# Attention's search spread in unequal parts over a step, and four buffers where the experts' rows are added

## The chip, the cores and the metric

One core of one Trainium2 chip runs the whole kernel. The metric is the time of one execution on the device in microseconds; lower is better. Three runs of the kernel before took 6582.45, 6589.72 and 6597.27 us; the median is 6589.72 us.

## What is computed

A prompt of 2048 tokens and eight sample tokens go through two layers of width 1024. Layer 0 has sparse attention: an indexer gives each query a score for each key, the best 256 keys are chosen (ties go to the earlier key), and attention runs over those alone. Layer 1 is a recurrent block. Behind each stands a mixture of 32 experts of which each token uses two. Only two places matter here:

```python
def block(args):                       # 128 queries of the prompt at a time
    sc = indexer_scores(qib, wib, ki, q_pos, k_pos)      # relu(q.k) per head, weighed, masked
    _, idx = lax.top_k(sc, topk)                         # topk = 256 keys
    valid = idx <= q_pos[None, :, None]
    return sparse_attend(qb, gather_rows(k, idx), gather_rows(v, idx), valid)

# the end of the experts: each token adds its two experts' rows
return jnp.zeros((N, D), x.dtype).at[st].add(yb[dest] * sw[:, None])
xp = xp + g2p[:, None, :] * hier_moe(...)                # both layers
y_prompt = rmsnorm(xp, norm_final_g)                     # behind the last
```

## The kernel before

The phases follow each other with a barrier of all engines between them: modulation, project, attend, the samples' index and attention, and then for each layer route, experts, combine, with the recurrent block between the layers. The change touches `phase_attend` (L485) and `phase_combine` (L2130).

**Attention** (`phase_attend`). The 16 tiles of 128 queries are taken in the order `TILE` (0, 1, 3, 5, ..., 15, 14, 12, ..., 2), so tile m has `L[m]` keys, 128 to 2048 and back to 384. The work is a pipeline written out by hand over `steps()`: in step i the engines do four tiles at once.

- Tile i: the attention proper. A step has `slots(i)` slots (2 to 32), each with two blocks of 128 keys for four heads. On TensorE `biased` and `scored_by_keys` (L952, L959) write scores, ScalarE takes the exponential (`exponentials`, L715), TensorE multiplies with the values one slot later (`with_values`, L970).
- Tile i+1: the row maxima. TensorE's `fill` (L980, L981) adds the hiding mask `hide` to a head's scores in one of two banks of `aux`, VectorE's `largest` (L795) reduces them. These units are shared over the first half of the slots, up to `middle(i)`.
- Tile i+2: the search for the 256th score. `cand` is found bit by bit in 31 rounds. For tiles of 1024 keys and more (`by_act`) ScalarE counts with a Sign and an accumulator (`weigh`, L752), and VectorE answers with the next bit (L848, L850); a round needs the answer of the one before. For narrower tiles VectorE counts itself (L835, L892, L894). Round 32 settles the last bit for ScalarE's tiles, and then `finish_search` (L896 to L919) counts the ties with a scan (L913) and writes `hide`. GpSimd copies it (`split_hide`, L664) for the step in which the tile is tile i.
- Tile i+3: the indexer's scores. TensorE's `index` (L1020) writes a pair of pieces into the two banks of `aux`, ScalarE rectifies them (L747) into one of four buffers, VectorE adds them up (L827). The pairs are shared over the second half of the slots.
- Tile i-1: the end. In the second slot VectorE's `normalise` (L807, L809) turns 1024 row sums per partition into reciprocals and multiplies; in the slot `middle(i)` TensorE projects (L992) and GpSimd adds the residual.

Before the change the 33 rounds are shared evenly over all slots of the step, and `finish_search` is one call behind the last round, in the last slot. Each engine works through its own list in the order in which the Python code writes it. In a slot TensorE does: scores, half of the units, values of the slot before, the other units, the projection in the slot `middle(i)`, and then the pairs. At the end of a step `turn_queries` (L1027) turns the queries of tile i+2, ScalarE copies them (L761) and GpSimd narrows them into `qTb` (`narrow`, L692), which the next step's units read together with `hide`. VectorE does in a slot: units, `normalise`, pairs, rounds.

**Combine** (`phase_combine`). For each of 17 tiles of tokens (the last has 8) GpSimd gathers two rows of 4 KB per token from `yb` (`indirect_dma_start`, L2186), SyncE loads `x` (L2171), ScalarE scales the first row (L2208), VectorE adds the second, multiplies with the gate and adds `x` (L2233, L2235, L2237), and ScalarE's queue stores `z` (L2204). `x`, `y` and `z` have two buffers. In layer 1 (`final`) the norm follows: ScalarE squares (L2215), GpSimd takes the root (`norm_rstd`, L246 and L247, with a `drain` between them) and VectorE multiplies (L2243). GpSimd's order in a turn of the loop is

```python
copy of the two indices into idxb, wait for it
gather(t, 0); gather(t, 1)
norm(t - 1)            # final only: add, drain, pow
```

In layer 0 SyncE first loads `rec_w_out` (4 MB), then the gates, then the `x` tiles.

## Time and profile before

| what | us |
|---|---|
| median of three runs | 6589.72 |
| profiled execution | 6591.56 |
| its span, first to last instruction | 6590.1 |
| attention's steps 0 to 15 (from 728 to 3008) | 2280 |
| combine of layer 0 (from 4339 to 4493) | 154 |
| combine of layer 1 (from 6384 to the end) | 206 |

The profile is one execution, taken by the hardware. A page of it lists busy time by engine and groups of instructions; the trace behind it can be asked for stretches (busy time of each engine in a window), for the order of events (timeline), and for groups with their waits. In a row PE is TensorE, PEld its weight loads, DVE VectorE, ACT ScalarE, POOL GpSimd, SP SyncE. "[5.35 <-DVE attend_mx L795]" is the time that the engine stood idle before the row and what ended it.

### The profile page before, as it was taken

The numbers are of one execution on the slowest core, as the hardware profiler recorded it, in microseconds if no ns is written. First come the engines' busy times: TensorE is split into PE (matmuls) and PEld (weight loads), VectorE is DVE, ScalarE is ACT, GpSimd is POOL, SyncE is SP. The second block draws the span as 40 slices with busy tenths as digits, with TensorE's granted clock in tenths as the row PEclk, the third lists the DMA queues.
The fourth block names the chain that finished last, engine by engine and source line by source line (L and its number), as shares of the span: only waits on it lengthen the run. The fifth ranks groups of instructions, "written<-read, shape, count | busy, mean of one in ns | idle before, by whom it ended". The sixth has DMA issues, their size and how long they took to land. (4 is left out here: it accounts for less than half of the span.)

```text
span 6590.1 us, 58804 instructions
## 1 busy us (share of the span) xinstructions
PE 4886.5 (74%) x16399; PEld 2498.9 (38%) x16453; DVE 2284.1 (35%) x4967; ACT 1865.8 (28%) x3244; POOL 696.1 (11%) x934
## 2 busy tenths in 40 slices
PE   7999456676787888887775599924888886579960
PEld 2444122222233333333234444413566564544430
DVE  1111554454345545653122301124444442321114
ACT  0111224455555553321121112212222231212211
POOL 0111211000000001111121100021000000100013
PEclk9999577888899999998886699966988896589985
DMA  6111100000000000004442677752000100447865
GB/s 239 52 49 37 53 12 16 10 8 12 12 5 12 7 12 12 15 19 150 128 150 88 245 284 280 261 210 95 32 25 19 38 13 17 147 140 272 292 217 163
DMA packets 177185, 634.10 MB, mean 96 GB/s; under 512 B 28920, under 2 KB 47737, under 8 KB 157930
## 3 DMA queue, kind: packets, MB, share of 16 engines
q1 hardware_dynamic: 112124, 408.37, 17.8%
q0 software_dynamic: 39072, 131.90, 6.0%
q10 hardware_dynamic: 25824, 91.88, 3.5%
q8 instruction: 74, 1.21, 0.1%
q14 instruction: 91, 0.75, 0.0%
HBM read 497.41 MB, written 134.72 MB: 96 GB/s over the span
## 5 line engine op out<-in xcount | busy, mean ns | idle before, releaser
L2112 PE MATMUL experts_ps_gu<-w_sb,experts_xT 128*128 x1504 | 679.6, 606 | 42.7 <-DMA w_sb<-moe_w_in 38.2
L970 PE MATMUL attend_po<-attend_PT,V 128*128 128x512 f32 x1088 | 564.8, 644 | 30.9 <-ACT attend_PT L715 18.5
L752 ACT ACTIVATE attend_passed<-attend_score,attend_cand 128x1024 bf16<-128x1024 f32 (+8 forms) x279 | 439.3, 1575 | 468.2 <-DVE attend_cand L850 443.9
L2621 PE MATMUL recurrent_psAB<-recurrent_hT,rec_w_in_sb 128*128 128x256 f32 (+1 forms) x2304 | 537.1, 393 | 10.6 <-ACT recurrent_hT L2416 10.6
L469 PE MATMUL project_pj<-project_w,project_hT 128*128 128x512 f32 (+2 forms) x1360 | 507.5, 530 | 6.6 <-ACT project_proj L385 5.5
L2621 PEld LDWEIGHTS recurrent_psAB<-recurrent_hT,rec_w_in_sb 128*128 128x128 f32 x2304 | 464.5, 215 | 77.1 <-issue 11.7
L795 DVE TENSOR_REDUCE attend_mx<-attend_aux 128x1 f32<-128x512 f32 (+3 forms) x640 | 365.3, 606 | 289.8 <-PE attend_aux L981 283.3
L2112 PEld LDWEIGHTS experts_ps_gu<-w_sb,experts_xT 128*128 128x128 f32 x1504 | 285.3, 195 | 372.0 <-issue 372.0
L981 PE MATMUL attend_aux<-attend_KTb,attend_qTb 128*128 128x512 bf16 (+3 forms) x640 | 236.2, 376 | 214.5 <-issue 198.3
L715 ACT ACTIVATE attend_PT<-attend_big 128x512 f32<-128x512 f32 x544 | 291.3, 586 | 238.9 <-PE attend_big L959 238.0
L2102 PE MATMUL experts_ps_y<-w_sb,experts_midT 128*128 x752 | 343.3, 600 | 11.4 <-issue 11.4
L959 PE MATMUL attend_big<-attend_qT,KT 64*128 64x512 f32 x1088 | 338.2, 701 | 0.0
L980 PE MATMUL attend_aux<-attend_hide,attend_identb 128*128 128x512 bf16 (+3 forms) x587 | 215.5, 371 | 162.4 <-DVE attend_mx L795 150.8
L970 PEld LDWEIGHTS attend_po<-attend_PT,V 128*128 128x128 f32 x1088 | 208.8, 205 | 317.2 <-issue 244.9
L469 PEld LDWEIGHTS project_pj<-project_w,project_hT 128*128 128x128 f32 (+1 forms) x1360 | 229.4, 185 | 261.7 <-issue 254.6
L1020 PE MATMUL attend_aux<-kiT,attend_qiT 64*128 64x512 f32 (+3 forms) x640 | 197.6, 701 | 160.8 <-ACT attend_relu L747 136.1
L980 PEld LDWEIGHTS attend_aux<-attend_hide,attend_identb 128*128 128x128 bf16 x640 | 64.2, 101 | 615.5 <-DVE attend_mx L795 337.2
L2066 DVE SCALAR_TENSOR_TENSOR experts_th<-experts_th,experts_ps_gu 128x256 f32<-128x256 f32 x94 | 39.6, 421 | 734.2 <-ACT experts_th L2045 734.2
L827 DVE SCALAR_TENSOR_TENSOR attend_score<-attend_relu,attend_wi,attend_score 128x512 f32<-128x512 f32 (+3 forms) x280 | 187.5, 671 | 282.3 <-ACT attend_relu L747 265.4
L2652 PE MATMUL recurrent_psO<-rec_w_out_sb,recurrent_g 128*128 128x512 f32 (+1 forms) x544 | 238.6, 599 | 28.6 <-DVE recurrent_g L2578 28.6
L992 PE MATMUL attend_aux<-attend_w_out,attend_oT 128*128 128x512 f32 x512 | 227.5, 603 | 16.5 <-DVE attend_oT L809 16.5
L2045 ACT ACTIVATE experts_th<-experts_ps_gu 128x256 f32<-128x256 f32 x94 | 36.0, 383 | 678.7 <-PE experts_ps_gu L2112 678.7
(426 smaller groups left out, 6124.3 us busy)
## 6 DMA issues: line engine op xcount, KB each, us to landing
w_sb<-moe_w_in SPq DMA_DIRECT2D x64, 2048.0 KB, 11.4
w_sb<-moe_w_in SPq DMA_DIRECT2D x64, 1024.0 KB, 8.8
yb_scratch<-experts_y ACTq DMA_DIRECT2D x94, 512.0 KB, 8.6
index_slab<-ada_w_in SPq DMA_DIRECT2D x12, 2048.0 KB, 9.6
sample_V<-cache_v_in POOLq DMA_DIRECT2D x128, 128.0 KB, 2.4
sample_K<-cache_k_in SPq DMA_DIRECT2D x128, 128.0 KB
route_x<-xa_scratch SPq DMA_DIRECT2D x32, 512.0 KB, 4.5
hs_scratch<-route_h ACTq DMA_DIRECT2D x32, 512.0 KB, 4.8
```

Of the source, the lines that this page charges most:

```text
L469: last = pe.matmul(pj[0:rows, bank, 0:c1 - c0], hT[:, b, k, 0:rows], w[:, k, c0:c1], start=(k == 0), stop=(k == KC - 1))
L715: act.activation(PT[:, g % 4, :], big[:, g % 4, :], ACT.Exp).then_inc(exped, 1)
L752: act.activation(passed[:, 0:L[m]], score[:, m % 2, 0:L[m]], ACT.Sign, bias=threshold, accum_out=balance[:, :]).then_inc(balanced, 1)
L795: dve.tensor_reduce(mx[:, h, c:c + 1], aux[:, u % 2, 0:wide], AX.X, ALU.max).then_inc(maxed, 1)
L959: pe.matmul(big[:, g % 4, :], KT[r, n // 2, b * P:(b + 1) * P], qT[r, i % 3, n // 2 * GQ:(n // 2 + 1) * GQ, :].rearrange("p a q -> p (a q) ...
L970: pe.matmul(po[:, n % 2, :], V1[:, b, n, :], PT[:, g % 4, :], start=(b == 0), stop=(b == S[i] // NKV - 1)).then_inc(pv_done, 1)
L980: pe.matmul(aux[:, u % 2, 0:n], identb4[:, 0, :], hide[:, keys], start=True, stop=False)
L981: pe.matmul(aux[:, u % 2, 0:n], qTb[:, h, :], KTb[:, h // GQ // 2, keys], start=False, stop=True).then_inc(unit_filled, 1)
L2102: last = pe.matmul(ps_y[:, half, :], midT[:, k, :], w2[:, bass.ds(slot, 1), k, half * 512:half * 512 + 512].rearrange("p a n -> p (a n)"), ...
L2112: last = pe.matmul(ps_gu[:, u, :], xT[:, u, k, :], w1[:, bass.ds(slot, 1), k, :].rearrange("p a n -> p (a n)"), start=(k == 0), stop=(k == ...
L2621: last = pe.matmul(psAB[:, c % 2, part, 0:W], w_in[:, k, part * D + c * P:part * D + (c + 1) * P], hT[:, k, 0:W], start=(k == 0), stop=(k ...
L2652: last = pe.matmul(psO[0:rows, half, :], g[:, k, i * P:i * P + rows], w_out[:, k, half * 512:half * 512 + 512], start=(k == 0), stop=(k == ...
```

## The change

In attention the rounds get unequal weights over a step's slots (two in the first half, one in the second, none in the last slot or two), `finish_search` becomes four pieces of its own, `normalise` becomes five parts spread over the first half, and TensorE writes half of a slot's pairs ahead of the values. In combine the buffers go from two to four, the loops are written out, the copy of the indices goes, SyncE stores as well as loads, and GpSimd's root of tile t comes ahead of the gathers of tile t+4.

```diff
-        ROUNDS = 33
+        PIECES = 37
+        def pieces_at(i, s):
+            n = slots(i)
+            if not there(i + 2):
+                return range(0)
+            weight = [1] if n == 1 else [2 if k < middle(i) else 1 for k in range(n - 1)] + [0]
+            if n > 8:
+                weight[n - 2] = 0
+            done, of = sum(weight[:s]), sum(weight)
+            return range(PIECES * done // of, PIECES * (done + weight[s]) // of)
+
+        def normal_at(i, s):
+            if middle(i) <= 2:
+                return range(5) if s == min(1, middle(i)) else range(0)
+            return share_of(5, s, 1, middle(i))
...
-                            for r in share_of(ROUNDS, s, 0, slots(i)):
+                            for r in pieces_at(i, s):
                                 if r < 31:
                                     weigh(i + 2, r)
...
-                def normalise(i):
+                def normalise(i, part):
                     dve.wait_ge(o_copied, 16 * (i + 1))
-                    dve.reciprocal(total[:, :, :], total[:, :, :])
-                    dve.drain()
-                    dve.tensor_tensor(oT[:, :, :], oT[:, :, :], total[:, :, :], ALU.mult).then_inc(o_normed, 1)
+                    if part < 4:
+                        dve.reciprocal(total[:, 2 * part:2 * part + 2, :], total[:, 2 * part:2 * part + 2, :])
+                    else:
+                        dve.drain()
+                        dve.tensor_tensor(oT[:, :, :], oT[:, :, :], total[:, :, :], ALU.mult).then_inc(o_normed, 1)
...
                 def search(m, r):
-                    if by_act(m):
+                    if r > 32:
+                        finish_search(m, r - 33)
+                    elif all_chosen(m):
+                        return
+                    elif by_act(m):
                         search_with_act(m, r)
...
+                def finish_search(m, part):
...
+                    elif part == 0:
+                        if m:
+                            dve.wait_ge(split_done, 2 * m)
+                            dve.wait_ge(unit_filled, sum(U[:m]))
+                        counted(m, threshold, ALU.is_gt)
+                        dve.tensor_scalar(out, at, threshold, None, ALU.is_equal)
+                        dve.tensor_scalar(count[:, :], count[:, :], -float(TOPK), None, ALU.add)
+                    elif part == 1:
+                        dve.drain()
+                        dve.tensor_tensor_scan(passed[:, 0:w], out, out, count[:, 0:1], ALU.add, ALU.bypass)
+                    elif part == 2:
+                        dve.drain()
+                        dve.scalar_tensor_tensor(out, passed[:, 0:w], 0.0, out, ALU.is_gt, ALU.mult)
+                    else:
+                        dve.drain()
+                        dve.scalar_tensor_tensor(out, at, threshold, out, ALU.is_lt, ALU.add)
+                        dve.drain()
+                        dve.tensor_scalar(out, out, -BIG, None, ALU.mult).then_inc(hidden, 1)
...
-                        units = units_at(i, s)
+                        units, pairs = units_at(i, s), pairs_at(i, s)
+                        early = 0 if s == middle(i) else (len(pairs) + 1) // 2
                         for u in units[:len(units) // 2]:
                             fill(i + 1, u)
+                        for pair in pairs[:early]:
+                            index(i + 3, pair)
                         if s:
                             with_values(i, 2 * s - 2)
                             with_values(i, 2 * s - 1)
...
-                        for pair in pairs_at(i, s):
+                        for pair in pairs[early:]:
                             index(i + 3, pair)
```

```diff
+    DEEP = 4
-        idxb = sb("idxb", [P, 2, 2], I32)
+        x = sb("x", [P, DEEP, D])
+        y = sb("y", [P, DEEP, 2, D])
+        z = sb("z", [P, DEEP, D])
...
             @block.sync
+                def store(t, b, rows):
+                    sp.wait_ge(done if final else added, t + 1)
+                    out = (T["y_prompt"][t * P:t * P + rows] if rows == P else T["y_sample"]) if final else rows_at(dst, t, rows)
+                    sp.dma_start(out, z[0:rows, b, :]).then_inc(out_[b], 16)
+
+                for t, b, rows in tiles[:DEEP]:
+                    load(t, b, rows)
+                load_modulation(sp, T, l, 5, gate[:, 0], gate[:, 1], mod_in)
+                sp.dma_start(g_final[:, :], T["norm_final_g"].broadcast_to([P, D])).then_inc(mod_in, 16)
                 if not final:
                     for k in range(KC):
                         sp.dma_start(T["rec_w_out_sb"][:, k, :], ...)
+                for t, b, rows in tiles:
+                    if t:
+                        store(*tiles[t - 1])
+                    if t + DEEP <= NT:
+                        sp.wait_ge(added, t + 1)
+                        load(*tiles[t + DEEP])
...
             @block.gpsimd
+                for t, b, rows in tiles[:DEEP]:
+                    fetch(t, b, rows)
+                for t, b, rows in tiles:
+                    if final:
+                        norm(t, b, rows)
+                    if t + DEEP <= NT:
+                        pool.wait_ge(added, t + 1)
+                        fetch(*tiles[t + DEEP])
```

## Rows read from the trace of the kernel before

**Rows 1.** The page: busy time of each engine, share of the span, instructions
```profile
PE 4886.5 (74%) x16399; PEld 2498.9 (38%) x16453; DVE 2284.1 (35%) x4967; ACT 1865.8 (28%) x3244; POOL 696.1 (11%) x934
```

**Rows 2.** First slots of steps 1 to 15: us, busy by engine, PEclk, DMA share, GB/s
```profile
781.00:813.30 32.30, 8.46 (x28) 2.95 (x30) 25.21 (x73) 4.11 (x10) 3.29 (x4) 0.63 0.05 22
900.00:934.70 34.70, 10.21 (x33) 4.13 (x35) 22.15 (x53) 9.06 (x18) 3.71 (x4) 0.64 0.05 20
...
sum 331.20, PE 131.31 PEld 53.50 DVE 237.55 ACT 83.55 POOL 63.98; mean PE 8.75 PEld 3.57 DVE 15.84 ACT 5.57 POOL 4.27
```

**Rows 3.** Stretches: the other slots before `middle`, same steps (4, 6, 11, sum)
```profile
1607.90:1688.80 80.90, 65.53 (x242) 26.64 (x245) 45.97 (x92) 42.07 (x52) 3.76 (x2) 0.92 0.00 1
...
2565.40:2629.50 64.10, 50.44 (x204) 20.50 (x206) 51.07 (x110) 10.86 (x20) 0.13 (x1) 0.92 0.00 1
...
sum 826.30, PE 670.89 PEld 276.28 DVE 520.16 ACT 338.64 POOL 32.26; mean PE 44.73 PEld 18.42 DVE 34.68 ACT 22.58 POOL 2.15
```

**Rows 4.** The slots behind `middle`, same steps and columns: steps 6, 8, sum
```profile
1711.30:1795.50 84.20, 61.26 (x196) 21.78 (x196) 27.01 (x68) 56.99 (x85) 0.00 (x0) 0.86 0.02 5
...
2132.50:2201.70 69.20, 63.44 (x232) 23.23 (x232) 21.26 (x62) 52.71 (x88) 0.59 (x1) 1.00 0.04 14
...
sum 731.10, PE 585.88 PEld 217.08 DVE 275.17 ACT 465.90 POOL 12.92; mean PE 39.06 PEld 14.47 DVE 18.34 ACT 31.06 POOL 0.86
```

**Rows 5.** Timeline over the start of step 9: start us, us, instruction [idle before]
```profile
2201.92 2.21 POOL L692 CAST attend_qTb<-attend_qT 64x1024 bf16<-64x1024 f32 x2 [68.58 <-ACT attend_qT L761]
...
2215.72 0.59 DVE L919 TENSOR_SCALAR attend_hide<-attend_hide 128x1664 bf16<-128x1664 bf16 x1
...
2216.80 0.63 PE L981 MATMUL attend_aux<-attend_KTb,attend_qTb 128*128 128x512 bf16 x1 [16.12 <-issue]
...
2227.18 6.54 DVE L807 RECIPROCAL attend_total<-attend_total 128x1024 f32<-128x1024 f32 x1
...
2235.98 0.61 PE L980 MATMUL attend_aux<-attend_hide,attend_identb 128*128 128x512 bf16 x1 [5.35 <-DVE attend_mx L795]
```

**Rows 6.** Timeline in the first half of step 6: two rounds that follow each other
```profile
1643.21 2.00 ACT L752 ACTIVATE attend_passed<-attend_score,attend_cand 128x2048 bf16<-128x2048 f32 x1 [3.44 <-DVE attend_cand L850]
...
1645.34 0.15 DVE L848 TENSOR_SCALAR attend_step<-attend_balance 128x1 int32<-128x1 f32 x1 [2.16 <-ACT attend_passed L752]
...
1645.77 2.00 ACT L752 ACTIVATE attend_passed<-attend_score,attend_cand 128x2048 bf16<-128x2048 f32 x1 [0.46 <-DVE attend_cand L850]
```

**Rows 7.** Groups of attention by shape: busy us, mean ns | idle before
```profile
L752 ACT ACTIVATE attend_passed<-attend_score,attend_cand 128x1024 bf16<-128x1024 f32 x31 | 35.6, 1148 | 46.2 <-DVE attend_cand L850 43.1 <-DVE attend_cand L844 3.1
...
L835 DVE TENSOR_SCALAR_CACHE_REDUCE attend_passed<-attend_score,attend_cand 128x896 bf16<-128x896 f32 x32 | 36.7, 1146 | 3.3 <-issue 0.2
```

**Rows 8.** Stretches of combine in layer 0: its start, and the rest
```profile
4339.00:4362.00 23.00, 0.00 (x0) 0.00 (x0) 0.00 (x0) 2.29 (x2) 4.19 (x6) 0.50 0.95 360
4362.00:4490.00 128.00, 0.00 (x0) 0.00 (x0) 62.75 (x51) 17.21 (x15) 40.57 (x45) 0.50 0.67 240
```

**Rows 9.** Timeline of combine in layer 1: one of some 14 alike turns
```profile
6440.31 1.15 ACT L2208 ACTIVATE combine_y<-combine_y,share 128x1024 f32<-128x1024 f32 x1 [3.17 <-DMA combine_y<-yb_scratch,combine_idxb]
6440.39 0.56 POOL L247 TENSOR_TENSOR combine_rs<-combine_rs,power 128x1 f32<-128x1 f32 x1 [2.99 <-issue]
...
6441.95 2.04 POOL L2186 DMA_INDIRECT combine_y<-yb_scratch,combine_idxb  x1 [0.85 <-POOL combine_idxb L2182]
...
6444.29 0.93 POOL L2186 DMA_INDIRECT combine_y<-yb_scratch,combine_idxb  x1 [0.30 <-issue]
...
6452.65 1.15 ACT L2208 ACTIVATE combine_y<-combine_y,share 128x1024 f32<-128x1024 f32 x1 [3.81 <-DMA combine_y<-yb_scratch,combine_idxb]
6452.72 0.57 POOL L247 TENSOR_TENSOR combine_rs<-combine_rs,power 128x1 f32<-128x1 f32 x1 [3.61 <-issue]
```

**Rows 10.** Stretches of combine in layer 1: its start, and the even part
```profile
6385.00:6396.00 11.00, 0.00 (x0) 0.00 (x0) 0.00 (x0) 0.10 (x1) 4.01 (x5) 0.50 0.89 322
...
6417.00:6567.00 150.00, 0.00 (x0) 0.00 (x0) 64.10 (x52) 29.65 (x39) 49.14 (x64) 0.50 0.56 175
```

134 lines of the change are left out of this document (51 added, 83 removed).

## The prediction

> **What bounds the kernel now.** I read the page first: TensorE is busy for 74% of the span, no other engine for more than 35% [rows 1], so the time is TensorE's work plus what it waits for. The change touches three stages: attention (2280 us), and combine in both layers (154 and 206 us), where TensorE has nothing to do.
>
> For attention I asked for stretches by part of a step. In the first slots TensorE is busy for 131.3 of 331.2 us, so 199.9 us are idle [rows 2]; in the other slots before `middle` 155.4 of 826.3 are idle [rows 3]; behind `middle` 145.2 of 731.1 [rows 4]. The slots `middle` hold the projection and are nearly full.
>
> The timeline names the waits of step 9 [rows 5]. TensorE stands for 16.1 us until VectorE has written `hide` (2216.3), although GpSimd had `qTb` ready at 2204.1: 12.2 us are `finish_search`'s alone. Then VectorE's reciprocal (6.5 us) keeps the units' reductions back, and TensorE idles 5.35 us more. Its granted clock, a mean between the levels of 1.2 and 2.4 GHz, is 0.63 and 0.64 over such slots [rows 2]. Behind `middle` the limit of the wide steps is ScalarE: 57.0 of 84.2 us busy in step 6, whose rounds stand between a pair and its rectifying. Step 8 has 63.4 of 69.2 us of TensorE's own work there [rows 4].
>
> In layer 1's combine I looked for what releases each turn [rows 9]. The root's second instruction (L247) starts 0.08 and 0.07 us behind ScalarE's L2208, which waits for the gather's landing. GpSimd stood idle for 3.0 and 3.6 us before it, and no engine's work is named as what it waited for. So GpSimd's `drain` ends when the gathers issued before it have landed, and the next gathers follow the root: one tile's gathers in flight, 12.3 us in this turn, 11.7 on average over the twelve turns from 6428.7 to 6568.5, 175 GB/s over the stretch against 322 at its start [rows 10].
>
> **The change part by part.** The sum is made against the profiled execution, 6591.6 us; the median is 1.8 us lower.
>
> *First slots.* The search now ends one or two slots before the step does, so the units wait for `qTb` alone. Of the 199.9 us idle, steps 1 and 2 hold 48.3 [rows 2]. Of the other 151.6 I leave 3.5 a step (the wait for `qTb`: in step 9 the idle time of 16.12 us begins at 2200.7, and `qTb` is there at 2204.1 [rows 5]) in steps 3 to 13 and the 3.4 of steps 14 and 15: 110 gained. The clock should give 1 us a step, 11; step 2 gives 12. Against this stand the rounds added in the first slot (two in steps 2 and 3, one in most others, 1.7 to 2.6 us each): 25. Gain 108.
>
> *Other slots before `middle`.* The weights put 25 to 28 of the 37 pieces ahead of `middle`, where 16 of 33 rounds stood. Between two rounds of a slot VectorE waits for ScalarE: 2.56 us from one to the next at 2048 keys [rows 6], of which 2.00 are the Sign; at 1024 keys the Sign takes 1.15 [rows 7], so some 1.7. While it waits it reduces no units. The first round of a slot is hidden, each further one is paid as far as TensorE's own work doesn't cover it. Rounds per slot go from 4 to 6.5, 2.75 to 4.5, 2.06 to 3.3, 1.65 to 2.6 in steps 2 to 5: 3 to 9 slots times 1 to 2.6 rounds times 1.7 to 2.35 us is 13, 17, 19 and 21, of which the spread reciprocal and fuller clock give back some: 56 lost. In steps 6 to 10 (1.4 to 2.2 at most per slot) cover is larger: 5.5, 5.5, 2, 0 and a gain of 2, the reciprocal's 5.35 us included: 11 lost. Steps 11 to 13 search on VectorE alone, which is the bound there (51.1 of 64.1 us in step 11 [rows 3]); nine or ten more rounds of 1.15 us and two small ones, less the width's fall: 12, 10 and 8 lost. Step 14 gains 4. Loss 93; the bounds are 45 (the rounds fill VectorE's idle time) and 150.
>
> *Slots behind `middle`.* About five ScalarE rounds stay of fifteen. Ten rounds of 2.2 us are 22 us of ScalarE's time in step 6, whose TensorE idles 22.9 there. With half of the pairs ahead of the values, ScalarE gets its work sooner too. I take 13, 15, 12, 18, 21 and 13 for steps 2 to 7 and 4 for steps 8 to 10, less nothing for the four pieces of `finish_search`: VectorE is 27.0 of 84.2 us busy [rows 4] and four buffers of `relu` cover a scan. If that cover went, a piece of up to 4 us would hold a pair back in each step, 15 to 30 in all. Gain 96; bounds 20 and 125.
>
> *Steps 0 and 1.* All of step 0's 37 pieces now stand in its first slot, ahead of the pairs; the queries are turned only behind the pairs. `hide` is early, `qTb` late. Loss 8, between 20 and a gain of 5.
>
> Attention: 108 - 93 + 96 - 8 = 103. Because its large terms are of both signs and worked out from averages I take 95.
>
> *Combine, layer 0.* There is no root here, so four tiles are really in flight. The start moves 360 GB/s [rows 8], the rest 240. Some 39 MB (17 tiles of 2.1 MB, 4.2 of weights, 1 of gates) at 335 GB/s, between the two starts and nearer to the one with the same mix of queues, are 116 us; with 3 ahead and 7 behind, 126 in place of 152. Gain 26, between 8 (the two-deep pace kept behind the weights) and 33. GpSimd's two gathers (up to 2.04 us each [rows 9]) and VectorE's work (62.8 us for some 16 tiles, 3.9 each) stay under the 6.3 us of transfer.
>
> *Combine, layer 1.* Four tiles are fetched at once, 7.9 MB with `x` and gates, at 322 to 360 GB/s landed near 6409. From then on the root of tile t stands behind the gathers of tile t+3 that were issued one turn ago and have not landed. The `drain` waits for them as before. A turn becomes root 0.6, issue 2.04 + 0.3 + 0.93 and the same landing. Of the 1.0 us between the root's end and the first gather, 0.85 is the wait for the copy of the indices [rows 9], and it goes. Twelve turns of 10.8 us end at 6539, the last gather at 6546, and three tiles of VectorE work (64.1 us in 12.8 turns [rows 10], 5.0 each) with store end at 6566. Gain 24, bounds 10 and (if `drain` didn't wait) 80.
>
> Sum: 6591.6 - 95 - 26 - 24 = 6446.6; I say 6450.
>
> The gathers' issue shows a second price: 2.04 us where VectorE's two-input L2233 ran from 6441.79 on, 0.93 for the next [rows 9]. The Trainium skill ("SBUF — State Buffer", section "SBUF: two separate sides") says that a VectorE instruction with two SBUF inputs and a GpSimd instruction that reads SBUF lock each other out for a whole instruction. By it, with VectorE now fed from four buffers, both gathers of a turn could be held, 1.1 us more in each of twelve turns: the sum would be 6463 instead of 6450.
>
> **The rivals.**
>
> *A, as above*: 6450; 0.60. Its own range is 6405 to 6495.
>
> *B, the second halves don't open.* The pairs wait for each other in the two banks of `aux`, and what limits them is that handshake, not the rounds. For: in step 6 ScalarE is idle for a third of the stretch. Against: fifteen rounds of 2.2 us are 33 of ScalarE's 57.0 us there. The 96 shrink to 20: 6526; 0.20.
>
> *C, the root is free.* The `drain` waits only for the gathers' issue. For: the code puts the root first as if it mattered. Against: both roots of rows 9 start 0.07 to 0.08 us behind a landing. Layer 1's 35 MB at 322 GB/s, 109 us and 15 around them, end at 6510 instead of 6566: 6394; 0.10.
>
> *D, slower.* The crowded first halves. Each of 9.5 moved rounds is exposed in full (2.1 us) in each of twelve steps, 240 us, and B holds as well: 108 - 240 + 20 - 8 + 50 = -70, so 6662. It decides once a moved round costs over 1.5 us on average; for it speaks that VectorE serves rounds and units in one queue, against it that in step 6 TensorE is busy for 65.5 of 80.9 us with rounds in place. 0.04.
>
> *E, no change*: gains and losses of attention cancel and B's loss eats combine; 0.06 with its surroundings, of which 0.02 within 0.2%, about what a measurement of this kernel can tell from no change.
>
> **How the numbers follow.** The likeliest case gives 6450. A with its range, B and C span 6385 to 6535, which leaves some 2 in 10 out. Faster by over 0.2%: A, B, C and most of E, 0.93; within 0.2%: 0.02; slower: D and a rest of E, 0.05.
>
> **What would show it.** Right: first slots of 12 to 15 us in steps 6 to 10 with 4 us of idle, no reciprocal over 1.7 us, first-half slots of steps 3 to 5 longer than before by 2 to 3 us, second-half slots of step 6 near 5.5 us; layer 0's combine near 126 us at over 300 GB/s; in layer 1 L247 still starting as a gather lands, some 10.8 us apart. Wrong: idle time behind `hide` in a first slot, second halves of steps 3 to 7 as long as before, roots that start without a landing, or a first half of step 4 over 85 us.

## The result, and the profile after

The changed kernel takes 6382.45 us in the median of four runs (6380.61 to 6385.54), the kernel before, run beside it, 6586.09: a ratio of 0.9692 with a 95% interval of 0.9678 to 0.9707, 3.1% faster. The prediction was 6450 with a range from 6385 to 6535: right in direction and in its mechanisms, but the gain came out larger than its range allowed, if by 2.5 us only. The profiled execution took 6381.06 us against 6591.56, so 210.5 us went where I forecast 141.6.

By part, from the traces of the two profiled executions (slots are cut, here as in the prediction, at the first exponential of each):

| part | before | after | measured | forecast |
|---|---|---|---|---|
| step 0 | 53.1 | 79.6 | +26.5 | +8 (steps 0 and 1) |
| first slots, steps 1 to 15 | 331.0 | 194.8 | -136.2 | -108 |
| other slots before `middle` | 826.3 | 957.9 | +131.6 | +93 |
| slots `middle` | 338.7 | 309.3 | -29.4 | none |
| slots behind `middle` | 731.3 | 608.1 | -123.2 | -96 |
| attention | 2280.4 | 2149.8 | -130.6 | -103, taken as -95 |
| combine, layer 0 (to its last instruction) | 151.0 | 101.5 | -49.5 | -26 |
| combine, layer 1 | 205.8 | 168.2 | -37.6 | -24 |
| all else | 3952.9 | 3959.8 | +6.9 | none |

The forecasts of -108, +93 and -96 were for steps 2 to 15; steps 0 and 1 had the +8 between them. Cut in that way, the measured parts are -115.6 in the first slots, +94.0 up to and with `middle` (of which -29.1 in the slots `middle`), -122.0 behind it, and +12.9 in steps 0 and 1 together. They add up to -130.7.

The page's first line, to be read beside [rows 1]. TensorE has the same work (4882.5 us busy, 4 less than before); only its idle time has shrunk.

```profile
PE 4882.5 (77%) x16452; PEld 2506.2 (39%) x16453; DVE 2275.0 (36%) x5015; ACT 1870.2 (29%) x3244; POOL 699.7 (11%) x900
```

Stretches by part of a step, columns as in [rows 2]. First the first slots of steps 1 and 2 and the sum over steps 1 to 15, which answer to [rows 2]; then the other slots before `middle` of steps 4, 6 and 11 with their sum, for [rows 3]; then those behind `middle` of steps 6 and 8 with their sum, for [rows 4].

```profile
808.10:819.80 11.70, 8.99 (x29) 3.33 (x30) 5.99 (x9) 4.11 (x11) 3.01 (x4) 0.85 0.12 49
913.50:935.70 22.20, 9.47 (x34) 3.94 (x35) 8.13 (x24) 11.56 (x23) 3.52 (x4) 0.81 0.06 25
...
sum 194.80, PE 131.56 PEld 52.11 DVE 77.52 ACT 95.80 POOL 61.33; mean PE 8.77 PEld 3.47 DVE 5.17 ACT 6.39 POOL 4.09
...
1227.80:1323.30 95.50, 62.17 (x184) 23.73 (x183) 39.25 (x95) 45.16 (x61) 4.57 (x2) 0.79 0.00 0
...
1585.80:1681.30 95.50, 75.18 (x261) 29.59 (x260) 47.78 (x113) 60.93 (x71) 4.79 (x2) 0.93 0.00 1
...
2427.80:2502.00 74.20, 56.81 (x209) 21.41 (x207) 61.92 (x144) 10.83 (x20) 0.13 (x1) 0.91 0.00 1
...
sum 957.90, PE 744.01 PEld 291.62 DVE 575.23 ACT 471.60 POOL 42.35; mean PE 49.60 PEld 19.44 DVE 38.35 ACT 31.44 POOL 2.82
...
1697.20:1761.20 64.00, 55.25 (x195) 22.41 (x193) 38.89 (x61) 36.59 (x67) 0.00 (x0) 0.92 0.02 7
...
2051.80:2113.00 61.20, 60.20 (x232) 25.34 (x230) 32.20 (x57) 37.77 (x69) 0.59 (x1) 1.00 0.05 16
...
sum 608.20, PE 539.07 PEld 221.17 DVE 333.19 ACT 327.46 POOL 14.26; mean PE 35.94 PEld 14.74 DVE 22.21 ACT 21.83 POOL 0.95
```

In the first slots TensorE is busy for 131.6 us as before (131.3), so all 136 us were idle time. VectorE's busy time there fell from 237.6 to 77.5: `finish_search` (L910 to L919 of the kernel before, 99 us of it) and the last counts of the step before are gone from it. Behind `middle` ScalarE's fell from 465.9 to 327.5 and in step 6 the stretch shrank from 84.2 to 64.0. Before `middle` the opposite: step 4 went from 62.9 to 95.5 us, where I had put the alarm at 85. TensorE's granted clock there is 0.79, a mean between its two levels; it was 0.92.

The start of step 9, for [rows 5]: TensorE waits for `qTb` alone, 3.5 us in place of 16.1.

```profile
2113.23 2.21 POOL L709 CAST attend_qTb<-attend_qT 64x1024 bf16<-64x1024 f32 x2 [60.63 <-ACT attend_qT L778]
...
2115.49 0.61 PE L1007 MATMUL attend_aux<-attend_hide,attend_identb 128*128 128x512 bf16 x1 [3.50 <-POOL attend_qTb L709]
```

The first half of step 4, to be read beside [rows 6]. L769 is ScalarE's count, L867 and L869 VectorE's answer, L812 its reduction of a unit, L1007 TensorE's next unit. It is the last round of a slot: the count, its answer, and what follows.

```profile
1235.56 1.58 ACT L769 ACTIVATE attend_passed<-attend_score,attend_cand 128x1536 bf16<-128x1536 f32 x1 [0.46 <-DVE attend_cand L869]
...
1237.26 0.15 DVE L867 TENSOR_SCALAR attend_step<-attend_balance 128x1 int32<-128x1 f32 x1 [1.74 <-ACT attend_passed L769]
1237.49 0.16 DVE L869 SCALAR_TENSOR_TENSOR attend_cand<-attend_step,attend_cand 128x1 int32<-128x1 int32 x1
1237.57 1.81 DVE L812 TENSOR_REDUCE attend_mx<-attend_aux 128x1 f32<-128x512 f32 x3
...
1238.31 0.40 PE L1007 MATMUL attend_aux<-attend_hide,attend_identb 128*128 128x256 bf16 x1 [3.22 <-DVE attend_mx L812]
```

VectorE stands for 1.74 us until the count is there, though two units have been in their banks since 1235; only behind the round does it reduce them, and TensorE, both banks full, has waited for 3.22 us.

Combine as stretches: layer 0's start and its even part, for [rows 8]; layer 1's, for [rows 10].

```profile
4214.00:4238.00 24.00, 0.00 (x0) 0.00 (x0) 5.07 (x5) 3.44 (x3) 8.10 (x9) 0.51 0.97 365
4238.00:4300.00 62.00, 0.00 (x0) 0.00 (x0) 44.65 (x37) 12.63 (x11) 26.39 (x26) 0.50 1.03 417
...
6211.00:6222.00 11.00, 0.00 (x0) 0.00 (x0) 0.00 (x0) 0.00 (x0) 7.49 (x8) 0.50 0.89 313
...
6240.00:6350.00 110.00, 0.00 (x0) 0.00 (x0) 53.70 (x45) 25.25 (x33) 41.47 (x43) 0.50 0.59 209
```

Layer 0 moves 417 GB/s with all queues busy, layer 1 209. One turn of layer 1, for [rows 9]:

```profile
6246.03 1.15 ACT L2250 ACTIVATE combine_y<-combine_y,share 128x1024 f32<-128x1024 f32 x1 [2.95 <-DMA combine_y<-yb_scratch,dest]
6246.22 0.56 POOL L247 TENSOR_TENSOR combine_rs<-combine_rs,power 128x1 f32<-128x1 f32 x1 [6.88 <-issue]
...
6247.00 1.97 POOL L2230 DMA_INDIRECT combine_y<-yb_scratch,dest  x1 [0.22 <-issue]
...
6249.28 0.94 POOL L2230 DMA_INDIRECT combine_y<-yb_scratch,dest  x1 [0.30 <-issue]
...
6256.57 1.15 ACT L2250 ACTIVATE combine_y<-combine_y,share 128x1024 f32<-128x1024 f32 x1 [3.49 <-DMA combine_y<-yb_scratch,dest]
6256.76 0.56 POOL L247 TENSOR_TENSOR combine_rs<-combine_rs,power 128x1 f32<-128x1 f32 x1 [6.11 <-issue]
```

L247 still starts 0.19 us behind a landing, and the pair of rows issued at 6247.0 and 6249.3 is the very one that lands at 6256.6: with four buffers there is still one pair in flight.

### The profile page after: what moved, and what is told of

The parts are those of the page before. It is cut to its first block and busy times, and to the rows that moved or that the text cites. A ratio compares the mean times of both kernels' runs of the same rounds, so it can differ in the third digit from the quotient of the medians.

```text
span 6379.3 us, 58455 instructions
## 1 busy us (share of the span) xinstructions
PE 4882.5 (77%) x16452; PEld 2506.2 (39%) x16453; DVE 2275.0 (36%) x5015; ACT 1870.2 (29%) x3244; POOL 699.7 (11%) x900
## 5 line engine op out<-in xcount | busy, mean ns | idle before, releaser
L2659 PE MATMUL recurrent_psAB<-recurrent_hT,rec_w_in_sb 128*128 128x256 f32 (+1 forms) x2304 | 537.4, 393 | 10.6 <-ACT recurrent_hT L2454 10.6
L769 ACT ACTIVATE attend_passed<-attend_score,attend_cand 128x1024 bf16<-128x1024 f32 (+8 forms) x279 | 439.4, 1575 | 357.1 <-DVE attend_cand L869 333.3
L2659 PEld LDWEIGHTS recurrent_psAB<-recurrent_hT,rec_w_in_sb 128*128 128x128 f32 x2304 | 465.2, 216 | 76.7 <-issue 11.7
L1007 PE MATMUL attend_aux<-attend_hide,attend_identb 128*128 128x512 bf16 (+3 forms) x640 | 246.8, 389 | 291.0 <-DVE attend_mx L812 241.1
L812 DVE TENSOR_REDUCE attend_mx<-attend_aux 128x1 f32<-128x512 f32 (+3 forms) x640 | 365.2, 606 | 278.1 <-PE attend_aux L1008 270.7
L2096 DVE SCALAR_TENSOR_TENSOR experts_th<-experts_th,experts_ps_gu 128x256 f32<-128x256 f32 x94 | 39.6, 421 | 735.2 <-ACT experts_th L2075 735.2
L1007 PEld LDWEIGHTS attend_aux<-attend_hide,attend_identb 128*128 128x128 bf16 x640 | 65.0, 102 | 579.9 <-DVE attend_mx L812 446.5
L1047 PE MATMUL attend_aux<-kiT,attend_qiT 64*128 64x512 f32 (+3 forms) x640 | 183.0, 654 | 142.0 <-ACT attend_relu L764 111.7
```

What stands on the lines that cost most here:

```text
L769: act.activation(passed[:, 0:L[m]], score[:, m % 2, 0:L[m]], ACT.Sign, bias=threshold, accum_out=balance[:, :]).then_inc(balanced, 1)
L812: dve.tensor_reduce(mx[:, h, c:c + 1], aux[:, u % 2, 0:wide], AX.X, ALU.max).then_inc(maxed, 1)
L1007: pe.matmul(aux[:, u % 2, 0:n], identb4[:, 0, :], hide[:, keys], start=True, stop=False)
L2659: last = pe.matmul(psAB[:, c % 2, part, 0:W], w_in[:, k, part * D + c * P:part * D + (c + 1) * P], hT[:, k, 0:W], start=(k == 0), stop=(k ...
```

## The experiments

Each kernel was run four times beside the kernel before, on one chip per group. Each ratio is against that group's own runs of the kernel before, whose medians went from 6571.9 to 6586.1 us. The table has its time, its ratio with the interval, and the parts from its own trace (us; the slots before `middle` and `middle` itself taken together, for a reason that the next section gives).

| kernel | time | ratio | step 0 | first | to `middle` | behind | attention | layer 0 | layer 1 |
|---|---|---|---|---|---|---|---|---|---|
| before | 6586.1 | 1 | 53.1 | 331.0 | 1165.0 | 731.3 | 2280.4 | 151.0 | 205.8 |
| changed | 6382.5 | 0.9692 (0.9678-0.9707) | 79.6 | 194.8 | 1267.2 | 608.1 | 2149.8 | 101.5 | 168.2 |
| attend_alone | 6441.8 | 0.9806 (0.9781-0.983) | 79.6 | 192.1 | 1267.0 | 607.6 | 2146.3 | 148.1 | 194.1 |
| early_end_alone | 6446.5 | 0.9802 (0.9783-0.9822) | 79.2 | 184.4 | 1219.4 | 733.4 | 2216.6 | 102.7 | 170.7 |
| even_rounds | 6401.1 | 0.9726 (0.971-0.9742) | 79.6 | 183.8 | 1190.4 | 720.1 | 2173.8 | 101.5 | 170.3 |
| pairs_behind | 6409.8 | 0.9744 (0.9728-0.976) | 80.2 | 198.4 | 1266.4 | 640.5 | 2185.5 | 101.1 | 171.1 |
| whole_reciprocal | 6413.8 | 0.9747 (0.973-0.9763) | 79.5 | 194.1 | 1295.5 | 611.5 | 2180.6 | 102.2 | 170.9 |
| even_late | 6356.2 | 0.9663 (0.9647-0.9679) | 80.1 | 195.3 | 1243.8 | 608.0 | 2127.2 | 100.9 | 168.8 |
| step0_halves | 6368.8 | 0.9686 (0.9669-0.9704) | 55.8 | 209.8 | 1266.1 | 607.6 | 2139.3 | 100.7 | 170.3 |
| rounds_between_units | 6303.5 | 0.9583 (0.9567-0.96) | 79.5 | 194.1 | 1190.2 | 614.2 | 2078.0 | 101.6 | 170.1 |
| even_between | 6346.9 | 0.966 (0.964-0.9679) | 79.7 | 184.5 | 1130.4 | 721.9 | 2116.4 | 101.6 | 169.2 |
| before_between | 6545.6 | 0.9952 (0.9936-0.9969) | 53.7 | 330.4 | 1130.9 | 735.2 | 2250.1 | 150.2 | 191.9 |
| root_no_drain | 6325.6 | 0.9623 (0.9607-0.9639) | 80.1 | 191.6 | 1265.2 | 610.4 | 2147.2 | 101.6 | 108.2 |
| two_deep | 6472.2 | 0.9845 (0.9828-0.9861) | | | | | 2149.6 | 138.1 | 229.6 |
| three_deep | 6390.4 | 0.9712 (0.9695-0.9728) | | | | | 2150.0 | 111.3 | 172.6 |
| five_deep | 6377.3 | 0.9695 (0.9679-0.9711) | | | | | 2149.6 | 101.5 | 167.0 |
| weights_first | 6389.8 | 0.9715 (0.9698-0.9732) | | | | | 2149.9 | 110.2 | 170.3 |
| gathers_first | 6379.3 | 0.9698 (0.9682-0.9714) | | | | | 2150.4 | 101.2 | 168.8 |
| two_deep_no_drain | 6398.1 | 0.9725 (0.9709-0.9741) | | | | | 2147.4 | 137.8 | 153.4 |
| all_four | 6219.5 | 0.9457 (0.9441-0.9472) | 55.9 | 212.8 | 1164.6 | 614.4 | 2047.6 | 102.2 | 114.2 |

Attention repeats within 4 us wherever its code is the same. Layer 1's combine with the code of before does not: 191.9, 194.1 and 205.8 us.

**Attention without the new combine** (`attend_alone`: `phase_combine` as before).

> The changed attention with the combine stages of the kernel before. Theory 1: the stages add up, so attention keeps its 2150 us (-130) and combine is back at 154 and 206 us: 6470 us, ratio 0.982. Theory 2: the stages are coupled (the clock granted to TensorE, transfers left over): attention differs from 2150 by more than 10 us, or the total from 6470 by more than 15.

Attention at 2146.3 us is what the first theory said. The total, 28 us under 6470, is outside its 15 and so by its words a sign of the second. The parts say where the 28 are: some 15 in the two combine stages, which came out at 148.1 and 194.1 in place of the 151.0 and 205.8 of the kernel before, 3.5 in attention, 6 in stages that no edit touched, and 3 between profiled executions and medians. That two of these stages have the code of before and came out shorter fits the spread of layer 1's combine above; it doesn't show a coupling, nor rule out a small one.

**GpSimd's drain.** First the semaphore in its place:

```diff
-                def link(_):
-                    pool.drain()
+                link = Chain(pool, linked)     # then_inc(linked, 1); wait_ge(linked, n)
```

> The changed kernel, but between the two instructions of the root GpSimd waits for the first one's own semaphore in place of a drain. Theory 1: the drain also waits for the landing of the gathers issued before it, so only one pair of gathers is in flight. Without it layer 1's combine falls from 167 to 105-125 us, no L247 starts at a landing, total 6325-6340. Theory 2: the turn is bound by something else that ends at the same time (the weighing in ScalarE's order): layer 1 stays at 160-170 us, total 6378-6388. Layer 0 has no root: 105 us by both.

Layer 1 falls to 108.2 us and the whole to 6325.6: the first theory, inside its numbers. A turn takes 5.05 us (twelve, from L247 at 6242.1 to L247 at 6302.7), and the transfers move 367 GB/s. The timeline of one turn, and the stretch:

```profile
6246.73 0.34 POOL L246 TENSOR_TENSOR combine_rs<-combine_ss,power 128x1 f32<-128x1 f32 x1
6247.10 1.23 DVE L2278 TENSOR_TENSOR combine_z<-combine_z,combine_gate 128x1024 f32<-128x1024 f32 x1
6247.15 1.59 POOL L247 TENSOR_TENSOR combine_rs<-combine_rs,power 128x1 f32<-128x1 f32 x1
...
6248.93 1.55 POOL L2230 DMA_INDIRECT combine_y<-yb_scratch,dest  x1 [0.18 <-issue]
```
```profile
6235.00:6295.00 60.00, 0.00 (x0) 0.00 (x0) 58.16 (x49) 26.23 (x36) 48.80 (x47) 0.50 0.94 367
```

L247 follows L246 at once; with the drain GpSimd stood idle for 4.5 to 6.9 us between them in the turns of the changed kernel. VectorE, busy for 58.2 of 60 us, is now the bound, beside DMA at 0.94.

Then the depth and the order (`DEEP` = 2, 3, 5; `norm` behind `fetch` in GpSimd's loop; `rec_w_out` ahead of the first `x`):

```diff
-    DEEP = 4
+    DEEP = 2                                  # two_deep; 3 and 5 in the others
```
```diff
                 for t, b, rows in tiles:       # gathers_first, and with DEEP = 2
-                    if final:                  # and no drain two_deep_no_drain
-                        norm(t, b, rows)
                     if t + DEEP <= NT:
                         pool.wait_ge(added, t + 1)
                         fetch(*tiles[t + DEEP])
+                    if final:
+                        norm(t, b, rows)
```

> The changed kernel with two buffers of x, y and z in place of four. Theory 1: in layer 0 the depth is what counts, so its combine goes from 105 back to 135-150 us; in layer 1 the drain holds one pair of gathers in flight at either depth, so it stays at 167-175 us. Total 6412-6440. Theory 2: depth counts in both: layer 1 is back at 195-206 us, total over 6450.

> The changed kernel with rec_w_out (4 MB) in front of the first x tiles in layer 0, as before the change. Theory 1: the 105 us of layer 0 are the bytes at some 400 GB/s, and the order only moves the weights: 105 to 108 us, total 6382-6386. Theory 2: the x tiles that no longer stand behind 4 MB of weights are a part of the gain: 113-120 us, total 6390-6398.

> The changed kernel with three buffers in combine. Two buffers gave 138 us in layer 0 and 230 in layer 1. Theory 1: in layer 1 what two buffers lack is that the root of tile t, which needs tile t+1 landed, stands ahead of the gather of tile t+2; with three the gather of t+3 follows it while t+2 is on its way, but the drain then waits for t+2: layer 1 at 166-175 us as with four, layer 0 at 105-112, total 6380-6395. Theory 2: each buffer counts in layer 1: 185-205 us there, total over 6400.

> The changed kernel, four buffers, with the next gathers in front of the root as in the kernel before, and the drain kept. Theory 1: at four buffers the ring issue, landing, drain's end, root, issue is the same from either side, so layer 1 stays at 163-176 us, total 6375-6392. Theory 2: the root in front is what brings the shorter turn: 185-205 us, total over 6398.

> Two buffers, the gathers in front of the root, and a semaphore in place of the drain. Theory 1: with neither the drain nor the root between them two pairs of gathers overlap as in layer 0 (138 us at this depth): layer 1 at 138-165 us, layer 0 at 138, total 6385-6415. Theory 2: at two buffers the landing bounds the turn whatever the order: over 190 us, total over 6440.

> The changed kernel with five buffers in combine. Layer 0 took 138, 111 and 101.5 us with two, three and four. Theory 1: at four the bytes bound it, 100-102 us, layer 1 168-172, total 6378-6386. Theory 2: the depth still counts: layer 0 at 94-98 us, total 6372-6378.

Three of the six went with their first theory: gathers_first, two_deep_no_drain and three_deep. five_deep has the first theory's 101.5 us in layer 0, which decides between its two, but its layer 1 (167.0) and its total lie 1.0 and 0.7 us under that theory's numbers. Layer 0 takes 138, 111, 101.5 and 101.5 us with two, three, four and five buffers: depth is most of its gain, and four are enough. In the even part of five_deep's layer 0 the transfers run as in the changed kernel:

```profile
4236.00:4298.00 62.00, 0.00 (x0) 0.00 (x0) 44.66 (x38) 13.78 (x12) 25.23 (x24) 0.50 1.03 416
```

The order of the weights is worth 8.7 us (110.2), between the numbers of both theories. What remains between 138.1 and the 151.0 of before is for the unrolled loops, the copy of the indices, the queues and that order together; I did not take them apart, and the order's 8.7 us were measured with four buffers, not with two.

two_deep fell under neither theory in layer 1: 229.6 us, more than before. Its timeline:

```profile
6342.99 0.18 POOL L246 TENSOR_TENSOR combine_rs<-combine_ss,power 128x1 f32<-128x1 f32 x1 [9.32 <-ACT combine_junk L2259]
...
6343.49 1.24 POOL L247 TENSOR_TENSOR combine_rs<-combine_rs,power 128x1 f32<-128x1 f32 x1 [0.31 <-issue]
...
6344.91 1.55 POOL L2230 DMA_INDIRECT combine_y<-yb_scratch,dest  x1 [0.18 <-issue]
```

The root of tile t waits for a Square that ScalarE runs behind the weighing of tile t+1, so tile t+1 has landed and nothing is in flight: here the drain takes 0.31 us. The next rows are fetched only then, and no transfer overlaps VectorE's and ScalarE's work. That one instruction pair so shows both of the drain's prices: 0.31 us with nothing in flight, 4.5 to 6.9 with a pair under way. With two buffers layer 1 takes 24 to 38 us more than with the code of before; the timeline puts it on the root in front, but no run has two buffers, the drain and the gathers in front, so that is not shown by itself. At four buffers the root's place is worth nothing (gathers_first 168.8, changed 168.2), since the drain closes the same ring from either side. Two buffers without drain, gathers first, take 153.4: 15 less than four with it.

**The parts of attention, one undone at a time.**

```diff
-            weight = [1] if n == 1 else [2 if k < middle(i) else 1 for k in range(n - 1)] + [0]
+            weight = [1] if n == 1 else [1] * (n - 1) + [0]                 # even_rounds
-                        early = 0 if s == middle(i) else (len(pairs) + 1) // 2
+                        early = 0                                           # pairs_behind
-            return share_of(5, s, 1, middle(i))
+            return range(1) if s == min(1, middle(i)) else range(0)         # whole_reciprocal
...
-                    if part < 4:
-                        dve.reciprocal(total[:, 2 * part:2 * part + 2, :], total[:, 2 * part:2 * part + 2, :])
-                    else:
+                    if part == 0:
+                        dve.reciprocal(total[:, :, :], total[:, :, :])
```

early_end_alone has all three of these edits.

> The changed kernel with weight 1 for every slot but the last or the last two (weight 0), so the early end of the search stays and the crowding of the first halves goes. Theory 1 (the terms on record): a round moved ahead of the middle costs there what it gives behind it; the slots before the middle fall from 958 to 850-890 us, those behind it rise from 608 to 660-700, attention ends within 15 us of 2150, total 6370-6400. Theory 2: the unequal weights are a part of the gain: attention 2170-2200 us, total 6400-6435. Theory 3: they are a loss, hidden by the rest: attention under 2130, total under 6365.

> The changed kernel with every pair behind the values, as before the change. Theory 1: half of the gain behind the middle comes from TensorE writing half of the pairs early, so that ScalarE gets them sooner: slots behind the middle +25 to +60 us, the rest unchanged, total 6407-6445. Theory 2: ScalarE's missing rounds are the gain and the order is free: within 8 us of the changed kernel, total 6374-6392.

> The changed kernel with the reciprocal in one piece of 6.5 us in the second slot. Theory 1: VectorE then owes rounds in that slot as well, and the whole 5 us come back in the second slot of each of steps 2 to 15, 40-65 us, total 6420-6445. Theory 2: what waits behind it is caught up in the next slots: 0-20 us, total 6380-6402.

> The changed kernel without three of attention's parts at once: weight 1 for every slot but the last ones, the reciprocal whole in the second slot, all pairs behind the values. What stays is the search's end one or two slots early, in four pieces (and the changed combine). One by one the three cost 24, 31 and 36 us. Theory 1: they add up, so attention is at 2230-2250 us (before 2280), total 6455-6480, and the early end by itself is worth 30-50 us although the first slots alone fall by over 120. Theory 2: the parts stand in for each other (each takes the same idle time), and without all three attention is at 2190-2225, total under 6450.

The unequal weights are worth 24.0 us (2173.8 against 2149.8), so the second theory: they cost 77 up to `middle` and 11 in the first slots, and bring 112 behind it. The early pairs are worth 35.7, of them 32.4 behind `middle`: the first theory. The reciprocal in parts is worth 30.8 us, between my two; 28.3 of them lie up to `middle`. early_end_alone went with the second theory (2216.6 us, total 6446.5): undone one by one the three parts cost 24.0, 35.7 and 30.8 us, 90.5 in all, undone together 66.8, so they partly take the same idle time. The early end by itself brings 63.8 of the 130.6 us: 146.6 in the first slots, against 54.4 up to `middle` (more pieces in fewer slots) and 26 in step 0. Its slots behind `middle` are as long as before (733.4, 731.3).

**Where the weights should not be used, and step 0.**

```diff
-            weight = [1] if n == 1 else [2 if k < middle(i) else 1 ...
+            weight = [1] if n == 1 else [2 if k < middle(i) and i < 11 else 1 ...   # even_late
+            weight = [1] * n if n <= 2 else [2 if k < middle(i) else 1 ...          # step0_halves
```

> The changed kernel with even weights in steps 11 to 13 alone, where VectorE counts by itself. Theory 1: there VectorE is the bound ahead of the middle and has room behind it, so its rounds should not be moved: these steps go from 144.8, 120.0, 101.0 to 134.5, 113.6, 95.1 us as they did with even weights everywhere, attention 2125-2131, total 6357-6363. Theory 2: part of that came from the steps around them: under 12 us in all, total over 6368.

> The changed kernel with step 0's pieces half in each of its two slots. Theory 1: step 0 (79.6 us, before 53.1) holds its pairs and its queries back behind 37 pieces, and halves give most of it back: steps 0 and 1 from 185.0 to 160-170 us, total 6357-6368. Theory 2: VectorE has the same work either way and it comes back in step 1: 172-185 us, as before the change (172.1) or worse, total 6369-6383.

Even weights in steps 11 to 13 bring 22.6 us: the steps go from 144.8, 120.0 and 101.0 to 135.6, 112.2 and 94.8, the first theory, with a total 0.8 us under its numbers. Halves in step 0 bring 23.8 us there, of which 17.2 come back in step 1 (105.4 to 122.6): 178.4 us for both steps, the second theory. All of attention gained 10.5; what lies beyond these two steps' 6.6 is within the 4 us by which attention repeats.

**The wait of the units.** VectorE's list, ahead of `middle`, with the rounds of a slot behind each second unit or so in place of behind all of them; even_between has even weights as well, before_between is the same edit in the kernel before:

```diff
-                        for u in units_at(i, s):
...
+                        for k, u in enumerate(units):
                             largest(i + 1, u)
+                            if between:        # 0 < s < middle(i), slots(i) > 4
+                                for r in rounds[len(rounds) * k // len(units):len(rounds) * (k + 1) // len(units)]:
+                                    search(i + 2, r)
...
-                        if there(i + 2):
-                            for r in pieces_at(i, s):
+                        if there(i + 2) and not between:
+                            for r in rounds:
                                 search(i + 2, r)
```

> The changed kernel with VectorE's rounds of a slot ahead of the middle written between its units in place of behind them. Theory 1: the loss ahead of the middle (958 us against 826) is VectorE standing for ScalarE's counts while units wait, so units between the rounds fill that wait: slots before the middle fall to 870-925 us, total 6290-6345. Theory 2: the loss is the amount of work in VectorE's and ScalarE's queues, whatever its order: 945-970 us, total 6370-6395.

> The kernel before with that one edit: units between the rounds ahead of the middle. Theory 1: the wait stood there too, where 16 of 33 rounds lie ahead of the middle in place of 25 to 28: attention from 2280 to 2225-2255 us, total 6525-6560. Theory 2: with one round a slot or fewer, ScalarE's count was hidden, and the change brought the wait in: over 2268 us, total over 6568.

> The changed kernel with weight 1 for every slot but the last ones and units between the rounds ahead of the middle. Theory 1: what made a moved round dear was units waiting behind it; with that gone the unequal weights are worth more than the 24 us of the first trial: attention 2115-2150 us (with unequal weights and units between: 2078), total 6340-6375. Theory 2: with even weights the wait is gone as well and there is no more to choose between the two: attention under 2105, total under 6335.

All three went with the first theory by attention's time and the total (the slots before the middle alone fell to 797.6 us, under the forecast 870, because the cut at `middle` moved; with `middle` they went from 1267.2 to 1190.2): 71.8 us from order alone, 30.3 in the kernel before, and unequal weights worth 38.4 us (2116.4 to 2078.0) where they had been worth 24.0. The timeline of step 4 with the edit, and its stretch before `middle`:

```profile
1219.04 1.57 ACT L769 ACTIVATE attend_passed<-attend_score,attend_cand 128x1536 bf16<-128x1536 f32 x1 [0.45 <-DVE attend_cand L869]
...
1220.74 0.15 DVE L867 TENSOR_SCALAR attend_step<-attend_balance 128x1 int32<-128x1 f32 x1 [0.54 <-ACT attend_passed L769]
1220.97 0.16 DVE L869 SCALAR_TENSOR_TENSOR attend_cand<-attend_step,attend_cand 128x1 int32<-128x1 int32 x1
1221.05 0.42 DVE L812 TENSOR_REDUCE attend_mx<-attend_aux 128x1 f32<-128x256 f32 x1
1221.16 1.57 ACT L769 ACTIVATE attend_passed<-attend_score,attend_cand 128x1536 bf16<-128x1536 f32 x1 [0.45 <-DVE attend_cand L869]
```
```profile
1207.80:1268.30 60.50, 44.03 (x164) 16.91 (x166) 37.36 (x95) 44.82 (x61) 3.35 (x2) 0.95 0.00 0
```

While ScalarE counts, VectorE reduces, and its idle time ahead of the answer is 0.54 us here in place of 1.74 (1.80 and 1.40 ahead of the answers next to it). The stretch is 60.5 us in place of 95.5 at a granted clock of 0.95 in place of 0.79. With the slot `middle`, which the cut moves into, step 4 went from 117.7 to 90.1 us; it was 88.7 before the change. The waits over all of attention, TensorE's unit matmul for VectorE (us in total, times, longest), in the kernel before, in the changed kernel and with the edit:

```profile
PE attend_aux L980 <- DVE attend_mx L795: 149.6, 92, 12.4
```
```profile
PE attend_aux L1007 <- DVE attend_mx L812: 239.9, 123, 21.0
```
```profile
PE attend_aux L1012 <- DVE attend_mx L812: 151.8, 133, 20.9
```

In steps 11 to 13, where VectorE counts by itself and waits for nobody, the order cost 7 us (145.9, 124.0, 102.7 against 144.8, 120.0, 101.0).

**All that gained, at once.** Units between the rounds where ScalarE counts, even weights in steps 11 to 13, halves in step 0, no drain:

> The changed kernel with four edits at once: ahead of the middle units between the rounds where ScalarE counts, even weights in steps 11 to 13, step 0's pieces in halves, the root's wait on a semaphore in place of the drain. Theory 1: they touch different waits and add up: attention 2150 - 72 - 7 (the loss of the edit in steps 11 to 13 goes) - 22 - 10 = 2039 us, layer 1's combine 108, total 6205-6222. Theory 2: they share idle time: attention over 2060, total over 6235.

6219.5 us, 0.9457 of the kernel before and some 2.5% under the changed one: the first theory. Attention came to 2047.6 where the sum said 2039, and layer 1 to 114.2 where it said 108: the gains add up but for 9 and 6 us.

## Why the prediction was wrong by so little, and where

**Which terms failed.** The mechanisms held; sizes were wrong. Against the profiled execution the gain was 210.5 us where I said 141.6. Of the 69 us between, 23.5 are layer 0's combine, whose rate I took too low, and which is the one term that left its own bounds (49.5 against 33); 26 are the slots behind `middle`, where I priced steps 8 to 10 at 4 us, steps 11 to 13 at nothing and the early pairs with no number of their own; 8 are the first slots, 8 the discount, 13.6 layer 1's combine, and 3.4 the rounding of 6446.6 to 6450. Against them stand 6 us of losses taken too small and 7 in all else.

**What bounds it, right.** Idle time of TensorE went and its busy time stayed; `hide` stood on the path of the first slots and stands there no more; the drain waits for landings, so rival C fell: the roots are not free, though the time came out near C's. B, D and E fell with the stretches below: the second halves opened by 122 us where B had 20, and the first halves cost 94 where D had 240. root_no_drain shows the drain itself as the cause, which the prediction had argued from 0.07 us between two rows.

**First slots: -116 in steps 2 to 15, forecast -108.** The 3.5 us of waiting for `qTb` came as forecast. The other 20.6 us of the table's -136 are step 1's, which belong to the term of steps 0 and 1. The charge of 25 us for rounds added was too large: the unequal weights cost 11 there (even_rounds 183.8). The gain ahead of that charge was a little too large as well, 133 against the 127 that even_rounds shows in these steps.

**Up to `middle`: +94 in steps 2 to 15, forecast +93.** The table above says +132 before `middle`, and the slots `middle` -29, which I had not forecast. Both are one thing: ScalarE's exponentials run behind its rounds, so the slot's first exponential comes late, and the projection, which is TensorE's, lies partly before it. In step 5 it starts at 1483.7 us, the slot by my cut at 1491.8; before the change it was 1475.7 and 1480.2. rounds_between_units moves the cut the other way (797.6 and 392.6). The mechanism was right, units waiting behind a round that waits for ScalarE: order alone took 77 us out of this part. That the sum was right within 1 us is in part luck: steps 2 to 5 lost 68 us where I had 56, steps 6 to 10 nothing where I had 11; steps 11 to 13 lost 31, forecast 30. Step 4's alarm of 85 us went off for 95.5, without rival D behind it. Its granted clock fell from 0.92 to 0.79, where my term had the clock as a gain ("fuller clock"); what share of the loss that is, no run separates.

**Behind `middle`: -122 in steps 2 to 15, forecast -96.** Steps 2 to 7 gained 94 us where I had 92. What failed is the rest: steps 8 to 10 gained 21 where I had 4, and steps 11 to 13 gained 6 where I had none. In pairs_behind steps 8 to 13 take 17 of these 28 us back (14 in steps 2 to 7), so most of the missing gain is the early pairs, which I had named but not priced. My rows would have allowed more than 4: in steps 8 to 10 TensorE stood idle for 16 us behind `middle`. And I took its own work for a floor, which it was not: in step 8 it is busy for 60.20 us with 232 matmuls where it was 63.44 with as many [rows 4]. The early pairs are worth 32 over all slots behind `middle` with the rounds gone; with even weights the stretch loses only 13 by them and the reciprocal together (733.4 to 720.1), so the pairs' order counts most once the rounds are out of the way.

**Steps 0 and 1: +13, forecast +8.** Step 0 takes 26.5 us more and step 1 takes 13.6 less: `hide` early, the queries late, as forecast. Step 1's first slot fell from 32.3 to 11.7.

**The discount, 103 taken as 95.** It had no row behind it, and went the wrong way: the two gains were 34 us too small (8 and 26), the two losses 6 (1 and 5).

**Combine, layer 0: -50, forecast -26, bound 33.** This term failed by the largest share. The depth was right, the rate was not: I took 335 GB/s, between two starts of 322 and 360 [rows 8, 10], as if a start showed the ceiling. At 417 GB/s the same 39 MB take 94 us. The rows of a start are means over its ramp. The trace of the kernel before, cut more finely, already had some 400 GB/s (columns as in [rows 8]):

```profile
4339.00:4345.00 6.00, 0.00 (x0) 0.00 (x0) 0.00 (x0) 0.00 (x0) 3.25 (x6) 0.50 0.77 275
4345.00:4351.00 6.00, 0.00 (x0) 0.00 (x0) 0.00 (x0) 0.00 (x0) 0.94 (x1) 0.50 1.01 397
4351.00:4357.00 6.00, 0.00 (x0) 0.00 (x0) 0.00 (x0) 1.54 (x2) 0.00 (x0) 0.50 1.03 401
```

In the changed kernel the start's mean is 365, and from 4226 on it moves 414. So a stretch in which engines issue their first transfers bounds the rate from below, not from above. The Trainium skill ("Perfetto Trace Analysis", section "Roofline") says that a core running alone is bounded by its 16 DMA engines together, at some 435 GB/s, rather than by its share of memory; the trace agrees (417 and 416 GB/s at a DMA share of 1.03). An estimate by that page, 39 MB at 435 GB/s with the same 3 and 7 us around them, is 100 us, beside the 101.5 measured.

**Combine, layer 1: -38, forecast -24.** The form was right: L247 at a landing, one pair in flight. The turn measured 9.95 us (eleven from 6246.2 to 6355.7) against 10.8 forecast and 11.65 before; I had kept the landing of the profiled execution of before, and that execution was a slow one in this stage. The same twelve turns take 11.0 us each in attend_alone and 10.6 in before_between; less the 0.85 us of the copy, that is 10.2 and 9.7, to either side of the 9.95. So the term was right, and the 14 us above it are for the most part no gain: the code of before took 205.8 in the profiled execution and 194.1 and 191.9 in the two others, against which the gain is 26 and 24. Why its landings differ from run to run stays open.

**The lock.** Each turn's gathers are issued in 1.97 and 0.94 us, as before (2.04 and 0.93): only the first is held, so the 1.1 us a turn by which 6463 stood above 6450 did not come. The rule of the Trainium skill itself ("SBUF — State Buffer", section "SBUF: two separate sides") is seen elsewhere: L247, which reads SBUF, takes 0.56 us with VectorE idle in the changed kernel and 1.59 in root_no_drain beside VectorE's two-input L2278.

The sum of the measured parts is 6591.6 - 130.6 - 49.5 - 37.6 + 6.9 = 6380.8, the profiled time of the changed kernel within 0.3.

## What to carry to other kernels

When a step of one engine waits for another's answer, write the work that waits for nobody between question and answer: here that order alone was worth more (72 us) than the whole redistribution of rounds (24), which it made worth more in turn (38). Before adding buffers, ask what closes the ring: with GpSimd's drain between two instructions of a root, four buffers kept one pair of gathers in flight, and two buffers without the drain (153 us) beat four with it (168). And take a transfer rate for a bound only from a stretch in which the DMA share has stopped rising, not from a mean over its start (360 there, 417 later).

## What the runs showed that was not expected

- GpSimd's drain took 0.31 us with no gather in flight and 4.5 to 6.9 us with a pair of them, until it landed; a semaphore between the same two instructions took the stage from 168.2 to 108.2 us.
- One core moved 417 GB/s through loads, stores and gathers together, and 365 in the mean of the first 24 us of the same stage, of which the first 4 moved 275.
- The small L247 on one element per partition took 0.56, 1.24 and 1.59 us: the longer ones beside VectorE's two-input instructions.
- TensorE's granted clock went with its waits for the units: in step 4's first half it was 0.92 before, 0.79 after the change and 0.95 with units between the rounds.
